# Sample recurrence of a state-update layer: GpSimd or VectorE, in four parts between the steps of the chunks

## What is computed

```
def step(S, inp):
    rt, wt, kt, vt, kkt, at = inp
    sa = einsum('nhij,nhj->nhi', S, -kkt)
    S = S * wt[:, :, None, :] + sa[..., None] * (kkt * at)[:, :, None, :] + vt[..., None] * kt[:, :, None, :]
    return S, einsum('nhij,nhj->nhi', S, rt)
```

## Time and profile before

| What | Value |
|---|---|
| median of 3 runs | 3846.57 us (3811.41 to 3867.77) |
| the profiled execution, its own time | 3805.45 us |
| its span, from the first to the last instruction | 3803.4 us |
| TensorE busy | 3125.3 us, 82% of the span |
| VectorE busy | 1634.2 us, 43% |
| ScalarE busy | 952.7 us, 25% |
| GpSimd busy | 339.4 us, 9% |
| granted TensorE clock, mean | 0.89 of full speed |

### The profile page before, as it was taken

The page is one execution under the profiler, slowest core; times in us unless marked ns, Lnnn a source line. Parts: engine busy times, 40 slices in busy tenths (PEclk is TensorE's granted clock), DMA queues, the critical chain, the costliest instruction groups (busy, mean ns, idle before and its releaser), DMA issues. The chain is left out here.

```text
span 3803.4 us, 56033 instructions
## 1 busy us (share of the span) xinstructions
PE 3125.3 (82%) x22104; PEld 2870.6 (75%) x22104; DVE 1634.2 (43%) x2739; ACT 952.7 (25%) x1825; POOL 339.4 (9%) x222
## 2 busy tenths in 40 slices
PE   3999999999888348759989999999886942876796
PEld 2998999977578247749979898998765931875795
DVE  2432432276143865633243235215724356654422
ACT  3212432232113122222142234213221311221222
POOL 0100000000000034500001000000000001542000
PEclk8999999999879569969999999999997965987898
DMA  3323345322413000023223232542242310000431
GB/s 132 92 54 88 99 113 147 89 65 61 113 45 104 8 24 1 1 84 112 91 74 78 68 102 71 150 125 78 51 101 62 90 46 24 1 1 14 143 111 66
DMA packets 412987, 283.24 MB, mean 74 GB/s; under 512 B 44172, under 2 KB 385868, under 8 KB 408238
## 3 DMA queue, kind: packets, MB, share of 16 engines
q1 hardware_dynamic: 407374, 271.98, 25.7%
q10 hardware_dynamic: 5344, 7.60, 0.6%
HBM read 243.33 MB, written 36.18 MB: 73 GB/s over the span
## 5 line engine op out<-in xcount | busy, mean ns | idle before, releaser
L355 PE MATMUL acc<-h_hi,in_w_hi 128*128 128x272 f32 x3968 | 900.6, 309 | 37.8 <-DVE h_lo L658 18.7
L355 PE MATMUL acc<-h_hi,in_w_lo 128*128 128x272 f32 x3968 | 839.2, 294 | 0.0
L355 PE MATMUL acc<-h_lo,in_w_hi 128*128 128x272 f32 x3968 | 838.5, 293 | 0.0
L355 PEld LDWEIGHTS acc<-h_hi,in_w_hi 128*128 128x128 f32 x3968 | 644.5, 195 | 97.5 <-issue 46.0
L355 PEld LDWEIGHTS acc<-h_lo,in_w_hi 128*128 128x128 f32 x3968 | 643.1, 194 | 0.0
L355 PEld LDWEIGHTS acc<-h_hi,in_w_lo 128*128 128x128 f32 x3968 | 639.6, 194 | 0.0
L382 DVE TENSOR_TENSOR in_w_lo<-in_w_raw,in_w_hi 128x512 fp32r<-128x512 f32 x496 | 349.4, 709 | 526.0 <-ACT in_w_hi L378 523.6
L378 ACT CAST in_w_hi<-in_w_raw 128x512 fp32r<-128x512 f32 x496 | 303.9, 617 | 499.0 <-PE acc L355 421.1
L355 PE MATMUL out_acc<-mix_hi,out_w_hi 128*128 128x272 f32 x1024 | 214.6, 291 | 46.6 <-DVE mix_lo L717 46.6
L355 PE MATMUL out_acc<-mix_hi,out_w_lo 128*128 128x272 f32 x1024 | 213.7, 290 | 0.0
L355 PE MATMUL out_acc<-mix_lo,out_w_hi 128*128 128x272 f32 x1024 | 213.2, 290 | 0.0
(11 more groups left out here) (541 smaller groups left out, 4477.3 us busy)
## 6 DMA issues: line engine op xcount, KB each, us to landing
in_w_raw<-in_w_in SPq DMA_DIRECT2D x488, 256.0 KB, 2.9
region<-in_cache_sb_kv SPq DMA_DIRECT2D x128, 256.0 KB, 3.0
out_w_raw<-in_w_out SPq DMA_DIRECT2D x128, 256.0 KB, 2.8
regions<-in_cache_dsa SPq DMA_DIRECT2D x64, 160.0 KB, 2.1
region<-x_spill SPq DMA_DIRECT2D x8, 1088.0 KB, 11.6
x_spill<-region SPq DMA_DIRECT2D x32, 272.0 KB, 2.1
mix_spill<-mix SPq DMA_DIRECT2D x6, 1088.0 KB, 6.1
mix_back<-mix_spill SPq DMA_DIRECT2D x6, 1088.0 KB, 7.3
```

The costliest lines, as they stand in the source:

```text
L355: last = pe.matmul(self.acc[:, i % 2, c, 0:HALF_N], w[:, u % RING, t, :], part[:, f, HALF_N * c:HALF_N * c + HALF_N], start=first and w is ...
```

## The change

`advance` becomes a generator on VectorE. It does the same seven elementwise instructions and the two row sums, in four parts; `next(recurrence)` runs one part. The parts stand in VectorE's program at four places: behind the masks of `k_kappa` and `k_r` (where the first row sum was), behind the two sums `add(q, 11, ...)`, behind the two sums `add(q, 14, ...)`, and behind the two sums `add(q, 19, ...)`, ahead of the serial end. GpSimd keeps its two copies. The hand-over through the semaphore `reduced` goes; `stepped` is now VectorE's own, on which each part waits for its own instructions. The second row sum no longer stands between the two chunks of the serial end.

```
-    def advance(self, pool, step, reduced, t):
+    def advance(self, dve, step, t):
...
-        step.then(pool.tensor_tensor(Z, S, over_i(4), ALU.mult))
-        step(pool.tensor_tensor(S, S, over_i(1), ALU.mult))
-        pool.wait_ge(reduced, 1)
-        step.then(pool.tensor_tensor(Z, over_j(self.sa[:, :]), over_i(5), ALU.mult))
-        step.then(pool.tensor_tensor(S, S, Z, ALU.add))
-        step.then(pool.tensor_tensor(Z, over_j(self.mine[:, t, :]), over_i(2), ALU.mult))
-        step.then(pool.tensor_tensor(S, S, Z, ALU.add))
-        step.then(pool.tensor_tensor(Z, S, over_i(0), ALU.mult))
+        step.then(dve.tensor_tensor(Z, S, over_i(4), ALU.mult))
+        step(dve.tensor_reduce(self.sa[:, :], Z, AX.X, ALU.add))
+        step.then(dve.tensor_tensor(S, S, over_i(1), ALU.mult))
+        yield
+        step.then(dve.tensor_tensor(Z, over_j(self.sa[:, :]), over_i(5), ALU.mult))
+        step.then(dve.tensor_tensor(S, S, Z, ALU.add))
+        yield
+        step.then(dve.tensor_tensor(Z, over_j(self.mine[:, t, :]), over_i(2), ALU.mult))
+        step.then(dve.tensor_tensor(S, S, Z, ALU.add))
+        yield
+        step.then(dve.tensor_tensor(Z, S, over_i(0), ALU.mult))
+        dve.tensor_reduce(self.y[:, t, :], Z, AX.X, ALU.add)
+        yield
...
                     for q in range(2):
                         done[q](spread(pool.tensor_copy, mats["kappa"][:, q], k.kr[:, :, c + q, 0, :]))
-                    for q in range(2):
-                        done[q].wait()
-                    samples.advance(pool, Steps(pool, stepped), reduced, c // 2)
...
-                    dve.wait_ge(stepped, 1)
-                    dve.tensor_reduce(samples.sa[:, :], samples.tmp[:, :, :], AX.X, ALU.add).then_inc(reduced, 1)
+                    recurrence = samples.advance(dve, Steps(dve, stepped), c // 2)
+                    next(recurrence)
                     for q in range(2):
                         keep(q, 10, "n4T", 3)
                     for q in range(2):
                         add(q, 11, "d", 0, mats["d"][:, q])
+                    next(recurrence)
                     for q in range(2):
                         add(q, 13, "d", 3, mats["d"][:, q])
                     for q in range(2):
                         add(q, 14, "d", 0, mats["d"][:, q])
+                    next(recurrence)
                     for q in range(2):
                         keep(q, 16, "rT", 3)
...
                     for q in range(2):
                         add(q, 19, "total", 3, mats["r1"][:, q])
-                    for q in range(2):
-                        if q == 1:
-                            dve.wait_ge(stepped, 7)
-                            dve.tensor_reduce(samples.y[:, c // 2, :], samples.tmp[:, :, :], AX.X, ALU.add)
+                    next(recurrence)
+                    for q in range(2):
                         dve.wait_ge(advanced, 4 * q + 2)
```

More of the change, by code:

```diff
@@ L2292, in rwkv_chunks @@
         made, by_v, by_s, by_p = (k.signals[2 * i:2 * i + 2] for i in range(4))
-        advanced, advanced_v, advanced_s, stepped, reduced = k.signals[8:13]
+        advanced, advanced_v, advanced_s, stepped = k.signals[8:12]
         def spread(copy, dst, src):
```

## The result

The changed kernel takes 3878.03 us as the median of 20 runs, the kernel before 3844.96 as the median of 20. The ratio is 1.0162, with a 95% interval from 1.0129 to 1.0194: 1.6% slower, some 62 us, and less than 2%. The ratio leaves disturbed runs out, on both sides, and so differs from that of the medians, which lie 33 us apart; the profiled execution of the changed kernel (3913.05 us, span 3911.2) is one of those.

What follows compares the result with a forecast made beforehand. No engine is full; the TensorE, VectorE, TensorE chain sets stage length. 2.7 + 2.37 = 5.07 us a stage, times eight 41 us (26 to 55), on the 3846.57 median gives 3887 us, 1.0% slower; range 3840 to 3930.

Steps and rivals of the forecast that it cites:

- The stall at L2503: VectorE's addition pair waits for whole GpSimd instructions, 5.00 us each; with GpSimd idle, 1.20 in place of 9.86 us.
- Rival 3: L2503's 5.00 us has another cause, so the pair keeps its 9.86 us: +99 us, 3946; chance 0.02.
- What the stall was worth: TensorE's wait before the product of `r2T`: 7.22 us standing still plus 1.80 lost at 1.2 GHz, -9.0 a stage.
- What the four parts land: Delays on TensorE's path at the four places in a stage: 4.64, 3.55, 1.72 and 2.37 us.
- What is late next: TensorE takes `x_mat`'s products first, ending 9.91 us later, so the product of `r2T` begins about 2.7 later than before.
- The clock: TensorE's clock in the new gaps: a stage loses 3.27 us with no fall, 5.07 with one, 6.87 with two.
- I take one: One clock fall a stage, priced as the one before, because the other new gaps are mostly shorter: 5.07 us a stage.
- My own bound for two falls: Two clock falls in each of the eight stages: 6.87 us a stage, 55 us slower.
- Rival 1: All four parts fit into VectorE's idle time: -9.0 us a stage, -72 us, 3774 us; chance 0.05.
- Rival 2: Clock falls at the first part's gap, staying low until `x_mat`: 12.3 us a stage, 98 us, 3945; chance 0.11.
- a sign of a clock that stays low: Expected sign in the new trace: a stage over 73 us would mean a clock that stayed low.
- the 66 to 70 us that I gave: Expected length of the chunk stages in the new trace, some 66 to 70 us.

Runs made afterwards that it cites:

- Experiments 1: Kernel before, recurrence still on GpSimd; addition r1 reads r from PSUM, ahead of the copy of rT: stages 439.4 us, ratio 0.9906.
- 2: Kernel before, addition r1 ahead of the copy of rT but with both inputs still from SBUF: stages 505.7 us.
- experiment 3: Changed kernel without the samples' recurrence, its nine VectorE instructions a stage not issued: stages 438.0 us.
- experiment 7: Changed kernel with unused TensorE products added in three waits, for the first, second and fourth parts: stages 35.4 us shorter than with the change, median 3891.85 us.
- experiment 6: Changed kernel with only the first part's first product moved ahead of the copy of block: stages 21.2 us less than with the change.
- experiment 4: Changed kernel with the same nine VectorE instructions in eight places a stage, not four: stages 450.4 us, ratio 0.9851.
- 5: Changed kernel with the fourth part moved behind chunk 0's state update: stages 37.3 us less than with the change, ratio 1.0196.

## Why the prediction was right, and where its size was off

The forecast was 3887 us, 41 us slower, with bounds of 26 and 55; the stages became 57.5 us longer, and the ratio says 62. Direction and mechanism held; the size was 1.4 to 1.5 times the forecast, above the upper bound. That the median, 3878.03, lies 9 us from the forecast is luck: the medians lie only 33 us apart, and runs of one kernel scatter by more than that. By its steps:

- **The stall at L2503** was GpSimd's, as read from the rows. Experiments 1 and 2 show it: one input from PSUM, 0.69 us; both from SBUF in the same place, 3.96. The Trainium skill, "SBUF — State Buffer", section "Who interferes with whom", states that a VectorE instruction with two SBUF inputs contends with a GpSimd instruction that reads SBUF, and that one with at most one SBUF input, outside the modes that take two ports, does not; the runs agree, with these two numbers. Rival 3 falls.
- **What the stall was worth.** I reckoned 7.2 us of standing still and 1.8 of clock, 9.0 a stage. Against experiment 3, the floor without the recurrence, it was 9.2.
- **What the four parts land.** I reckoned 4.64 + 3.55 + 1.72 + 2.37 = 12.28 us a stage. With the clock kept up (experiment 7) the stages lie 12.0 above the floor. The gaps at parts 1 and 3 came out at 4.45 and 1.52. The one at part 2, 2.84 and not 3.5, is shorter because the fall at part 1 makes TensorE late for it: in experiment 6 it is 3.35 in the two stages without that fall and 2.3 to 3.1 in the six with it. At part 4 it is 3.02, where I wrote "over 4".
- **What is late next.** TensorE did take the products of `x_mat` first: in stage three the last two of them start at 1629.80, and the product of `r2T` at 1630.03, without a gap.
- **The clock** is the term that was mis-sized. I wrote "I take one", one fall a stage; all eight stages show two, at part 1 and at part 4, and together they cost 4.4 us (experiment 7). My sum, with one fall before and one after, put the difference at nothing. With 12.0 for the parts, 4.4 for the clock and 9.2 back, the measured 7.2 of a stage is divided up. My own bound for two falls, 55 us, was close. The reason that I gave, that only the longest gap is long enough, does not hold: part 4's gap of 3.0 us and one of 2.1 us in experiment 6 let the clock fall, while one of 2.8 at part 2 did not.
- **Rival 1** falls for the change, but experiment 4 shows what it had right: the work does fit into VectorE's idle time, at 1.5 us a stage above the floor, in eight places and not in these four.
- **Rival 2** did not happen at its place: behind part 1 the clock was back at 1.00 well before `x_mat` in all eight stages. Something like it happened behind part 4: there it stayed down for over 12 us in two stages, the ones of 73.4 us, which I had named as a sign of a clock that stays low. Of the other six, five are above the 66 to 70 us that I gave.

Two kernels beat both: GpSimd with r1 from PSUM (stages 439.4 us, ratio 0.9906) and VectorE in eight places (450.4 us, 0.9851). Their timed intervals overlap, so the 11 us between them are shown by the stages alone.

## What to carry to other kernels

Before work is moved off an engine because it holds up another, look at what the held-up instruction reads: here one input from PSUM in place of SBUF gave 72.4 us in the stages, and the move in its better order 61.4. Work put into an in-order engine costs by the place: nine instructions of 2.3 us cost 1.5 us a stage in eight places, nearly all alone, and 16.4 where two or three stand together ahead of a step for which TensorE waits. And ask of each new gap on TensorE not only what it delays but what the clock loses behind it: here the clock fell at two gaps of four, and their length did not tell which.

## What the runs showed of the hardware

TensorE can be busy without a break and stay at 1.2 GHz. In the profiled execution of the changed kernel a stretch of the projections, which the change does not touch, runs like this; behind it are the same stretches of the kernel before:

```profile
550.00:600.00 50.00, 50.00 (x231) 50.00 (x230) 6.29 (x10) 6.24 (x11) 0.00 (x0) 0.50 0.39 114
600.00:650.00 50.00, 50.00 (x232) 50.00 (x231) 7.58 (x12) 6.27 (x11) 0.00 (x0) 0.50 0.27 82
```

```profile
550.00:600.00 50.00, 50.00 (x434) 50.00 (x434) 12.23 (x19) 11.03 (x20) 0.00 (x0) 1.00 0.58 168
600.00:650.00 50.00, 50.00 (x405) 48.57 (x406) 11.61 (x22) 9.88 (x21) 0.00 (x0) 1.00 0.47 134
```

231 products in 50 us in place of 434, for over 100 us, with TensorE busy in every one of them. The execution's span is 108 us above the one of before. The stages explain 57.5; the first of them starts at 1443.14 in place of 1382.32, 61 us later, and this stretch lies in that time; the rest of the span is some 11 us shorter. The kernel without the recurrence has the same stretch at the same place (232 and 231 products), the run with the filled gaps has one in its second layer and none of that length in its first, and experiments 4 and 5 have none there, with the same code up to that place: it comes and goes. Runs of one kernel scatter by 100 us and more. That this is what they scatter by is likely, and the mean clock of the fastest and the slowest of the changed kernel's 20 runs fits (0.892 at 3843.48 us, 0.868 at 3934.96), but where in them it fell no trace shows. The Trainium skill, "TensorE: Matmul & The Clock Gate", section "Part 1: The HAM clock gate", says that the clock is set by how busy TensorE has been just before; these rows, and the 12 us behind part 4, do not agree, and here the measurement decides.
